# Experts' scatters that add onto a stored residual, one in flight at a time, and a last stage that loads one row a token

## What is computed

```python
h = h + hybrid_mixer(rmsnorm(h, norm_mix_g), ...)
ffn = hier_moe(rmsnorm(h, norm_ffn_g), ...)      # 32 experts, two for each token, weighted
h = h + ffn
return rmsnorm(h, norm_final_g)[:, N_META:]
# in hier_moe: rows of each expert gathered, silu(x Wg) * (x Wu) Wd, times the slot's weight, and
out = zeros.at[slot_tok].add(ys * slot_w[:, None])   # two rows of sum for each token
```

## Time and profile before

| | |
|---|---|
| median of 3 runs | 1511.28 us (1510.02 to 1511.88) |
| the profiled execution | 1510.35 us; span 1508.5 us, so 1.85 us lie around the span |
| experts, from the first gather to the last scatter | 1115 to 1460 us of the span |
| last stage, from its first DMA issue | 1467 to 1508.5 us |

### The profile page before, as it was taken

How to read it: one execution, slowest core, us unless ns; L and a number is a source line. 1 busy time by engine, 2 the same in 40 slices (tenths; PEclk the granted TensorE clock), 3 DMA queues, 4 the chain that set the end, 5 groups by cost and what they waited for, 6 DMA issues and landing times. The chain is left out here.

```text
span 1508.5 us, 21819 instructions
## 1 busy us (share of the span) xinstructions
PE 1367.9 (91%) x7326; PEld 1117.2 (74%) x7327; DVE 1030.4 (68%) x1950; ACT 664.6 (44%) x1179; POOL 420.6 (28%) x476
## 2 busy tenths in 40 slices
PE   5989999999999989999999889999539999999950
PEld 4779888789989758888888778899536777777730
DVE  4448999999960567777888754432547777877727
ACT  4347323322121157777777641221016666666612
POOL 1100335322121043555555114100021333333214
PEclk9999999999999999999999989999759999999985
DMA  5030411123223002103442073221457999999718
GB/s 206 29 141 36 143 57 56 57 78 101 90 83 108 19 1 56 24 1 106 100 100 72 1 229 126 97 89 65 170 223 274 346 366 354 357 370 383 272 54 324
DMA packets 88702, 217.40 MB, mean 144 GB/s; under 512 B 24784, under 2 KB 49904, under 8 KB 76328
## 3 DMA queue, kind: packets, MB, share of 16 engines
q1 hardware_dynamic: 77200, 190.45, 36.3%
q0 software_dynamic: 9216, 16.80, 3.0%
q10 hardware_dynamic: 2200, 9.02, 1.5%
HBM read 193.05 MB, written 44.73 MB: 158 GB/s over the span
## 5 line engine op out<-in xcount | busy, mean ns | idle before, releaser
L421 PE MATMUL ps<-hHi,g_lead 128*128 128x512 f32 (+2 forms) x480 | 184.7, 385 | 8.7 <-DVE g_rest L818 7.5
L315 DVE TENSOR_SCALAR_CACHE_REDUCE mask<-score,cand 128x272 bf16<-128x272 f32 (+6 forms) x224 | 185.5, 892 | 4.6 <-DVE cand L334 4.4
L2219 DVE TENSOR_TENSOR w_rest<-wgu,w_lead 128x1024 fp32r<-128x1024 f32 x128 | 156.0, 1223 | 45.1 <-ACT w_lead L2166 43.9
L422 PE MATMUL ps<-hLo,g_lead 128*128 128x512 f32 (+2 forms) x480 | 183.9, 383 | 0.0
L423 PE MATMUL ps<-hHi,g_rest 128*128 128x512 f32 (+2 forms) x480 | 183.0, 381 | 0.0
L1310 DVE TENSOR_TENSOR pL<-ps,pH 128x512 fp32r<-128x512 f32 (+3 forms) x224 | 124.6, 572 | 51.4 <-ACT pH L1245 48.8
L2166 ACT CAST w_lead<-wgu 128x1024 fp32r<-128x1024 f32 x128 | 134.4, 1055 | 38.0 <-PE ps L2112 38.0
L732 POOL TENSOR_TENSOR g_rest<-g_raw,g_lead 128x2048 fp32r<-128x2048 f32 x12 | 55.6, 4633 | 300.8 <-ACT g_lead L588 300.8
L1245 ACT CAST pH<-ps 128x512 fp32r<-128x512 f32 (+3 forms) x224 | 106.2, 493 | 58.0 <-PE ps L1191 57.8
L2110 PE MATMUL ps<-w_lead,x_lead 128*128 128x512 f32 x256 | 114.2, 446 | 6.0 <-DVE w_rest L2219 6.0
L2132 PE MATMUL ps<-wd,hmT 128*128 128x512 f32 x256 | 115.3, 593 | 1.6 <-DVE hmT L2242 1.0
(11 more groups left out here) (349 smaller groups left out, 3399.1 us busy)
## 6 DMA issues: line engine op xcount, KB each, us to landing
wgu<-in_w_exp_gate SPq DMA_DIRECT2D x32, 1024.0 KB, 7.6
wgu<-in_w_exp_up SPq DMA_DIRECT2D x32, 1024.0 KB, 12.6
wd<-in_w_exp_down SPq DMA_DIRECT2D x32, 1024.0 KB, 12.4
g_raw<-in_w_in SPq DMA_DIRECT2D x16, 1024.0 KB, 5.6
gates_d<-stage SPq DMA_DIRECT2D x32, 256.0 KB, 2.0
gt<-gates_d SPq DMA_DIRECT2D x32, 256.0 KB, 3.1
rel_d<-rel_s ACTq DMA_DIRECT2D x1, 4672.0 KB
KR<-kb_d SPq DMA_DIRECT2D x16, 260.0 KB, 6.3
```

The lines of the kernel that those rows point to most:

```text
L315: return dve.tensor_scalar(mask[:, OFF[i]:OFF[i + 1]], score[:, OFF[i]:OFF[i + 1]], thr, 0.0, op, ALU.add, accum_out=cnt[:, i:i + 1])
L421: pe.matmul(dst, x[0], y[0], start=(k == 0), stop=False)
L422: pe.matmul(dst, x[0], y[1], start=False, stop=False)
L2219: dve.tensor_tensor(w_rest[u][:, :, 2 * part:2 * part + 2, :], wgu[u][:, :, 2 * part:2 * part + 2, :], w_lead[part][:, :, :, :].bitcast(F3 ...
```

## The change

`ys_d` shrinks to one row a token. In the projection stage SP stores each finished block of `h1` there, behind the store of `x2`, and waits for those stores at the end of the stage. The experts' scatters use the token as their row (`tok_i` in place of `dst_i`) and add onto what is there (`compute_op=ALU.add`). Since two experts may have the same token, a scatter now also waits until the scatter right before it has landed. The last stage loads one tensor, and both adds of DVE are gone.

```diff
-        ys_d = dram("ys_d", (2 * T, D), F32)
+        ys_d = dram("ys_d", (T, D), F32)
...
                         sp.dma_start(xn2_d[P * (b - 1):P * b, :], x2[(b - 1) % 2][:, :]).then_inc(s_xos[(b - 1) % 2], 16)
+                        sp.dma_start(ys_d[P * (b - 1):P * b, :], h1[:, b - 1, :]).then_inc(s_hd, 16)
                 for k in range(2):
                     sp.wait_ge(s_xos[k], 16 * NB // 2)
+                sp.wait_ge(s_hd, 16 * NB)
...
             def scatter(n, half, u, first):
                 if not first:
                     pool.wait_ge(ST[u % 2], half * 16)
-                pool.tensor_copy(dk[u % 2][:, :], dst_i[:, bass.ds(n, 1)]).then_inc(S["m_dk"], 1)
+                pool.tensor_copy(dk[u % 2][:, :], tok_i[:, bass.ds(n, 1)]).then_inc(S["m_dk"], 1)
                 pool.wait_ge(S["m_dk"], n + 1)
                 pool.wait_ge(S["m_ya"], n + 1)
                 pool.wait_ge(S["m_yd"], n + 1)
+                if u % 2 == 1:
+                    pool.wait_ge(ST[0], half * 16 + 16)
+                elif not first:
+                    pool.wait_ge(ST[1], half * 16)
                 pool.sem_inc(S["m_ask"], 1)
                 pool.indirect_dma_start(out=ys_d, out_offset=bass.IndirectOffsetOnAxis(ap=dk[u % 2][:, 0:1], axis=0),
-                                        in_=ye[u % 2][:, :], in_offset=None,
-                                        bounds_check=2 * T - 1, oob_is_err=False).then_inc(ST[u % 2], 16)
+                                        in_=ye[u % 2][:, :], in_offset=None, bounds_check=T - 1,
+                                        oob_is_err=False, compute_op=ALU.add).then_inc(ST[u % 2], 16)
...
             for b in range(NB):
-                for k, t in enumerate((ya, yb)):
-                    sp.dma_start(t[b][:, :], ys_d[T * k + P * b:T * k + P * (b + 1), :]).then_inc(s_ls[b], 16)
+                sp.dma_start(ya[b][:, :], ys_d[P * b:P * (b + 1), :]).then_inc(s_ls[b], 16)
...
-                    act.wait_ge(s_a2, b + 1)
+                    act.wait_ge(s_ls[b], 16)
...
-                    act.activation(sq[:, :], h1[:, b, :], ACT.Square, accum_out=ss[:, b:b + 1]).then_inc(s_sq, 1)
+                    act.activation(sq[:, :], ya[b][:, :], ACT.Square, accum_out=ss[:, b:b + 1]).then_inc(s_sq, 1)
...
-                dve.scalar_tensor_tensor(fo[b % 4][:, :], h1[:, b, :], rstd[:, b:b + 1], gf[:, :], ALU.mult,
+                dve.scalar_tensor_tensor(fo[b % 4][:, :], ya[b][:, :], rstd[:, b:b + 1], gf[:, :], ALU.mult,
                                          ALU.mult).then_inc(s_o, 1)
 
             for b in range(NB):
-                dve.wait_ge(s_ls[b], 32)
-                dve.tensor_tensor(ya[b][:, :], ya[b][:, :], yb[b][:, :], ALU.add).then_inc(s_a1, 1)
-                dve.wait_ge(s_a1, b + 1)
-                dve.tensor_tensor(h1[:, b, :], h1[:, b, :], ya[b][:, :], ALU.add).then_inc(s_a2, 1)
-                if b:
-                    finish(b - 1)
-            finish(NB - 1)
+                finish(b)
```

More of the change, by code:

```diff
@@ L1446, in hybrid_layer @@
                   "s_t2a", "s_t2d", "s_rp", "s_rl", "s_rb"])
+        s_hd = sem("s_hd")
         s_xrs, s_xos = [s_xr, sem("s_xr1")], [s_xo, sem("s_xo1")]
@@ L2332, in _ @@
                     pool.tensor_copy(tk[0][:, :], tok_i[:, bass.ds(b + NE, 1)]).then_inc(S["o_tk"], 1)
-                    pool.tensor_copy(dk[0][:, :], dst_i[:, bass.ds(b + NE, 1)]).then_inc(S["o_dk"], 1)
+                    pool.tensor_copy(dk[0][:, :], tok_i[:, bass.ds(b + NE, 1)]).then_inc(S["o_dk"], 1)
                     pool.wait_ge(S["o_tk"], b + 1)
@@ L2343, in _ @@
                                             out_offset=bass.IndirectOffsetOnAxis(ap=dk[0][:, 0:1], axis=0),
-                                            in_=ye[0][:, :], in_offset=None,
-                                            bounds_check=2 * T - 1, oob_is_err=False).then_inc(S["o_st"], 16)
+                                            in_=ye[0][:, :], in_offset=None, bounds_check=T - 1,
+                                            oob_is_err=False, compute_op=ALU.add).then_inc(S["o_st"], 16)
                     pool.wait_ge(S["o_st"], b * 16 + 16)
@@ L2407, in final @@
     ya = [at(f"fa{b}", [P, D], F32, R_K + 8192 * b) for b in range(NB)]
-    yb = [at(f"fb{b}", [P, D], F32, R_K + 8192 * b + 4096) for b in range(NB)]
     gf = at("gfin", [P, D], F32, R_K + 65536)
@@ L2411, in final @@
     fo = [at(f"fo{k}", [P, D], F32, R_K + 73728 + 4096 * k) for k in range(4)]
-    s_g, s_a1, s_a2, s_sq, s_v, s_r, s_o = map(sem, ["f_g", "f_a1", "f_a2", "f_sq", "f_v", "f_r", "f_o"])
+    s_g, s_sq, s_v, s_r, s_o = map(sem, ["f_g", "f_sq", "f_v", "f_r", "f_o"])
     s_ls = [sem(f"f_l{b}") for b in range(NB)]
```

## The result

The changed kernel takes 1524.09 us (median of 4 runs, 1522.90 to 1525.29) against 1510.65 us for the kernel before in the same comparison: a ratio of 1.0089 with an interval of 1.0071 to 1.0106. It is slower by 0.9%. The prediction said 1503 us and faster; the sign was wrong, while its range (1493 to 1548) held the time. The profiled execution took 1522.9 us with a span of 1521.1 us.

The account below looks back on a forecast made before the run. PE was taken to pace the experts, DMA engines close behind, and a DVE-ACT-POOL chain the last stage. -15.5 + 0 + 5.2 + 2.4 = -7.9 us from 1510.35 gave 1502.4, as a median 1503; range 1493 to 1548.

Parts of the forecast that it names:

- Last stage: Final stage, with fewer loads and DVE passes: -15.5 us taken, with ends of -17.3 and -8.5 us.
- the DMA limit: Last stage: 8.9 MB of loads, gain and stores at 415 GB/s take 21.5 us, to 1490 plus a landing.
- (d): Last stage held by its DMAs, -8.5 in place of -15.5: 1509 us; chance 0.08 with its neighbours.
- Stores of `h1`: Projection stage: eight more DMAs on SP, 0.33 us of issue each, hidden: 0 us, up to +1.
- The wait: Experts' scatters in series: met today with only 0.5 us to spare, period 9.6 us against 10.05.
- What an add costs: Experts' scatters: +1.0 us under load, landing 9.6, period 10.6 us, costing +5.2 us after slack.
- the prediction's own formula: Experts: scatter period is landing + 0.98; its excess over 10.05 us, 25 times, less 8.5 us of slack, is lost.
- The end: Last scatters: absorbed delay is won back, quiet landing 4.6 us; tail +2.4 us (+0.8 to +3.8).
- Rival (a): Experts: the scatter series becomes the bound, +2.1 us a scatter, period 11.7, 1533 us; chance 0.27, up to 1545.
- point of decision: Experts: from about +1.35 us a scatter on, the series' loss eats the last stage's gain.
- (e): Experts' DMA bandwidth: 10.8 us an expert, 19 us in all, about half swallowed by weights' lead; 1503 to 1506, no own chance.

Follow-up runs that it names:

- the wait-alone run: The kernel before with only the new wait put in, scatters still plain writes and the last stage as before: 1511.39 us, ratio 1.0003.
- the layout runs: Slots moved to other partitions: kernel before, spread, 1508.17 us; changed kernel, spread, 1495.17 us; changed kernel, whole groups of eight or four, 1527.89 and 1528.57 us.
- the two kernels with the spread: Kernel before and changed kernel, each with an expert's first 64 slots in partitions 0, 1, 4 and 5 of each eight: 1508.17 and 1495.17 us.

## Why the prediction was wrong, step by step

**Last stage: right, the last 1.6 us of it by luck.** -15.5 predicted, -15.7 measured; squares 2.0 us apart as laid out by hand, 25.75 us in all where "about 26" stood, first load landing 3.6 us after its issue. The steps laid out by hand gave -17.3, and -15.5 was a guess between them and the DMA limit. Of the 1.6 us between, 1.3 lie at one place: ACT waits 2.4 us for the second block's load, and the second `fo` starts 3.3 us after the first (1501.31 and 1504.62). The rival in which DMAs hold the whole stage (d) did not come.

**Stores of `h1`: right.** The last is issued at 1071.79 us, and the first expert's scatter starts at 1150.51, before at 1150.55. The DMA share of that stage rises from 0.23 to 0.32, with room to spare.

**The wait: right.** Alone it costs nothing, as the wait-alone run shows.

**What an add costs: mis-sized, and this decided the sign.** The step was "64 rows over 16 engines are 4 each, +0.7 us", with 0.3 us for POOL: +1.0 under load, landing 9.6. Measured are +1.6 and 10.2 us. Three things in it were off. By the layout runs and the shares of the last scatter 8 engines have some 8 real rows each. An adding row costs an engine more than one extra plain row: alone 0.46 us against 0.17, as shown above; under load, if a gathered row keeps the 0.17 us of the prediction, and gathered and scattered rows are equally many at 66 us a MB (0.27 us a 4 KB row), about 2 x 0.27 - 0.17 = 0.37 us (an estimate). The Trainium skill says of reduce-scatter that its add needs two source reads, which halve the rate ("Collectives: The Full Stack", section "Why ReduceScatter is half of AllGather"); this trace agrees in direction and is at or above that factor, 0.37 to 0.46 against 0.17 us a row. And POOL's share was taken as 0.3 us and is 0.6 (1.60 against 1.02). How the 1.6 us divide stays open: 8 x 0.20 + 0.6 would be 2.2 us, and between the two kernels with the spread, where the same sum gives 4 x 0.20 + 0.6 = 1.4, the landing grows by 2.3 (7.1 to 9.4). Quiet, the add costs 3.0 us (6.2 against 3.2) where 0.7 to 2.1 were pieced together.

With the right landing the prediction's own formula gives the measured delay: period 10.2 + 0.98 = 11.2 us, 1.13 over, 25 times 28.3; slack 7.9 us; 20.4 left, and PE ends 20.5 us later. That does not show that the series alone sets the pace, for without a series the last scatter still starts 19.7 us late.

**The end: wrong assumption.** "What was absorbed is won back at the end" took the 3.2 us quiet landing of a plain scatter. An adding one needs 6.2 + 1.0 = 7.2 us, and the last four intervals are 7.2 us on average (1453.21 to 1481.84), while PE's last two experts come 4.9 us apart (1466.76 and 1471.66). So 4.8 us of the backlog stay, and the last landing adds 3.0: 7.8 in place of +2.4.

Rival (a), 1533 at 27%, came nearest to the time, at +1.6 us a scatter in place of its +2.1, and past its own point of decision of +1.35. Its mechanism, the series, is one of the two limits; the other is what (e) had set too low.

## What to carry to other kernels

A partial indirect DMA (64 of 128 slots in use) loads the DMA engines unevenly; lay its rows so that each group of four partitions has its share, before counting DMA time. A DMA share of 0.95 that is a mean over 16 engines may mean that some are full and others not: compare landings of the same transfer after moving rows, and look at the share while one such transfer runs alone. Price an accumulating scatter at two to three times a plain one's engine time, and where it runs in series, take its quiet landing for the tail as well. Here the change pays once the rows are spread: 1495 us, against 1508 for the kernel before with the same spread and 1511 without it.

## What was not expected of the hardware

- The layout of slots over partitions is worth 28.9 us of 1524 at equal bytes, and the fast layout reaches a mean DMA share of 1.01 at 363 GB/s where the slow ones stop at 0.94 and 331 to 337 GB/s.
- An adding 4 KB row takes 0.46 us of an engine alone and an estimated 0.37 under load, against 0.17 for a plain one; its scatter lands in 6.2 us quiet against 3.2, and POOL needs 1.60 us against 1.02 to write it.
- Halving the bytes of each adding row gave back 27 of the 29 us that adding costs here (one execution).
- While one scatter of 57 rows runs alone, the mean DMA share is 0.51 with its rows in partitions 0 to 63 and 0.87 with them spread.
